# Triangular inverses of a chunked recurrence in packed 32x32 blocks on four row quarters, the inverse and its transpose both by TensorE

## The reference, cut to what matters

```
def _rwkv7_step(state, inp):
    r, w, k, v, kk, kka = inp
    sa = jnp.einsum('dbhvk,dbhk->dbhv', state, kk)
    state = state * w[..., None, :] - sa[..., :, None] * kka[..., None, :] + v[..., :, None] * k[..., None, :]
    y = jnp.einsum('dbhvk,dbhk->dbhv', state, r)
    return state, y
...
    xs = (orient(both(r)), orient(decay), orient(k_dir), orient(both(v)),
          orient(both(kk)), orient(kk[:, :, None, :] * a))
    state0 = jnp.zeros((N_DIRS, B, H, N, N), jnp.float32)
    _, ys = lax.scan(_rwkv7_step, state0, xs)
...
def _dilated_attention(q, k, v, window, dilation):
    s = jnp.einsum('bhrnqd,bhrnkd->bhrnqk', qb, kb).astype(jnp.float32)
    s = jnp.where(valid, s, -jnp.inf)
    m = jnp.max(s, axis=-1, keepdims=True)
    p = jnp.exp(s - m)
```

## Time and profile before

| | us |
|---|---|
| median of 3 runs | 1295.57 (1292.97 to 1296.23) |
| the profiled execution | 1297.45 |
| its span in the profile | 1295.4 |
| TensorE busy in it | 1230.7 |
| the stage: first chunk products to output projection | 917.16 to 1035.03 |

### The profile page before, as it was taken

One profiled execution on the slowest core, in us unless ns is written; L12 is line 12 of the kernel. 1 busy time (PEld: TensorE's weight loads), 2 busy tenths in 40 slices (PEclk: granted clock), 3 DMA queues, 4 the chain that ended last, 5 costly groups with the idle time before them and its releaser, 6 DMA issues.

```text
span 1295.4 us, 27192 instructions
## 1 busy us (share of the span) xinstructions
PE 1230.7 (95%) x11566; PEld 1153.2 (89%) x11566; DVE 586.2 (45%) x1057; ACT 617.9 (48%) x969; POOL 896.1 (69%) x689
## 2 busy tenths in 40 slices
PE   6999799999999999998899999999899988999997
PEld 6999689899998899997899998989898977999996
DVE  2533546742652222224545334458977444432333
ACT  5665434736744444445544445675322014544443
POOL 5988245686986999994799994867400013999992
PEclk9999999999999999999999999989999998999998
DMA  6555134454565556563555655434100022665561
GB/s 247 191 165 179 50 93 139 145 180 146 184 220 165 178 182 190 183 188 115 158 191 184 191 182 194 154 121 157 36 3 3 4 68 66 196 189 185 188 186 66
DMA packets 53256, 189.81 MB, mean 147 GB/s; under 512 B 6160, under 2 KB 7312, under 8 KB 53008
## 3 DMA queue, kind: packets, MB, share of 16 engines
q1 hardware_dynamic: 50256, 181.95, 43.9%
q10 hardware_dynamic: 2880, 6.12, 1.4%
HBM read 187.00 MB, written 1.05 MB: 145 GB/s over the span
## 4 chain that ended last, share of the span: by engine, by line
PE 83%; DVE 9%; ACT 5%; DMA 2%; issue 1%; POOL 0%; DVEq 0%; ACTq 0%
PE product L500 16%; PE product L502 16%; PE product L501 16%; PE bank L557 6%; PE bank L559 6%; PE bank L558 6%; PE product L1036 3%; PE bank L1036 3%; ACT weight_hi L2242 1%; PE product L587 1%; PE product L631 1%; PE bank L500 1%; DVE arena L1504 1%; PE bank L868 1%; PE bank L501 1%
## 5 line engine op out<-in xcount | busy, mean ns | idle before, releaser
L477 POOL TENSOR_TENSOR weight_lo<-raw_ring,weight_hi 128x512 fp32r<-128x512 f32 x684 | 890.6, 1335 | 375.3 <-ACT weight_hi L2242 344.1
L2242 ACT ACTIVATE weight_hi<-raw_ring 128x1024 fp32r<-128x1024 f32 x338 | 356.1, 1059 | 413.4 <-DMA raw_ring<-in_ffn_gu 108.1
L500 PE MATMUL product<-operand_B_hi,weight_hi 128*128 128x256 f32 x1104 | 312.3, 283 | 4.6 <-POOL weight_lo L477 4.6
L502 PE MATMUL product<-operand_B_hi,weight_lo 128*128 128x256 f32 x1104 | 311.3, 282 | 0.0
L501 PE MATMUL product<-operand_B_lo,weight_hi 128*128 128x256 f32 x1104 | 310.8, 282 | 0.0
L500 PE MATMUL product<-operand_A_hi,weight_hi 128*128 128x256 f32 x840 | 242.5, 289 | 14.2 <-DVE weight_lo L1353 10.8
L502 PE MATMUL product<-operand_A_hi,weight_lo 128*128 128x256 f32 x840 | 238.4, 284 | 0.0
L501 PE MATMUL product<-operand_A_lo,weight_hi 128*128 128x256 f32 x840 | 238.3, 284 | 0.0
L500 PEld LDWEIGHTS product<-operand_B_hi,weight_hi 128*128 128x128 f32 x1104 | 208.1, 188 | 7.9 <-issue 3.2
L501 PEld LDWEIGHTS product<-operand_B_lo,weight_hi 128*128 128x128 f32 x1104 | 207.9, 188 | 3.2
L502 PEld LDWEIGHTS product<-operand_B_hi,weight_lo 128*128 128x128 f32 x1104 | 207.9, 188 | 0.0
(11 more groups left out here) (355 smaller groups left out, 1571.1 us busy)
## 6 DMA issues: line engine op xcount, KB each, us to landing
raw_ring<-in_w_in SPq DMA_DIRECT2D x107, 512.0 KB, 3.5
raw_ring<-in_ffn_gu SPq DMA_DIRECT2D x88, 512.0 KB, 3.5
raw_ring<-in_ffn_down SPq DMA_DIRECT2D x44, 512.0 KB, 3.5
raw_ring<-in_w_mlp_up SPq DMA_DIRECT2D x32, 512.0 KB, 4.2
raw_ring<-in_w_mlp_down SPq DMA_DIRECT2D x32, 512.0 KB, 4.2
raw_ring<-in_w_out SPq DMA_DIRECT2D x16, 512.0 KB, 4.2
raw_ring<-in_w_branch_c SPq DMA_DIRECT2D x8, 512.0 KB, 3.4
raw_ring<-in_w_branch_a SPq DMA_DIRECT2D x8, 512.0 KB, 3.4
```

The source lines that it names most:

```text
L477: last = k.nc.gpsimd.tensor_tensor(k.wlo[:, slot, part], k.raw[:, slot, part], k.whi[:, slot, part].bitcast(F32), ALU.subtract)
L500: mm(ps, w_hi, op.hi[:, b, :], start=b == 0, stop=False)
L502: return mm(ps, w_lo, op.hi[:, b, :], start=False, stop=b == blocks - 1)
L2242: k.nc.scalar.activation(k.whi[:, slot, 0:w], k.raw[:, slot, 0:w], ACT.Copy).then_inc(k.s["hi_ready"], 1)
```

## The change

T and its transpose are kept only in their two diagonal 32x32 blocks (`HC` = 32) through levels 1 to 4, packed: partitions 0-31, 32-63, 64-95 and 96-127 hold the two halves of two heads, and a unit has 32 columns (`tc`, `uc` and the new `tt`, 256 columns in all instead of 512). A product of a level is now `quarters`: 8 units x 4 quarters = 32 matmuls of 32x32 by 32 columns. Level 5, which joins the two halves, is two products of `between_halves`, 16 matmuls each. `first_products` makes only one of the two triangular products, in pieces with 32 weight columns (`left_products`, 40 matmuls); the start of `tt` comes from it by a mask (L2108 in the new file) and an addition (L2110), the start of `tc` by a VectorE transpose in 32x32 blocks (L2099). The full 64x64 transpose `ttc`, which `solve` reads, is put together at the end: GpSimd fills it with zeros early, ScalarE copies the diagonal quarters after level 4 (`diagonal_halves`, 4 copies a chunk), VectorE the off-diagonal ones after level 5 (4 copies a chunk). Masks are stored for halves. Apart from that, attention's scores are made with the opposite sign, so that a minimum takes the place of a maximum and its negation, and the exponential has a scale of -1.

```diff
-    k.nt, k.tc, k.uc = ([units(9760 + 1536 * lane + 512 * n) for lane in range(2)] for n in range(3))
+    k.levels_half = k.masks.rearrange("p (d m t) -> p d m t", d=2, m=16)
+    half_units = lambda start: region(start, 8, HC)
+    k.nt = [units(9760 + 1536 * lane) for lane in range(2)]
+    k.tc, k.uc, k.tt = ([half_units(9760 + 1536 * lane + 512 + 256 * n) for lane in range(2)] for n in range(3))
     k.ttc, k.zaac, k.zaqc = ([units((12832, 15904, 18976, 6144)[j] + 512 * n) for j in range(NRC)] for n in range(3))
     k.zaqb = [units((14368, 17440, 20512, 22048)[j]) for j in range(NRC)]
...
+    pool.wait_ge(k.s["cb_made"], 1)
+    for j in range(NRC):
+        k.nc.gpsimd.memset(k.ttc[j], 0.0).then_inc(k.s["tt_zero"], 1)
...
+    def left_products(j):
+        bank = k.lane[j % 2][1]
+        for u in range(8):
+            lhs, rhs = feature(B_, j)(u), feature(A_, j)(u)
+            ahead = 0 if u < 4 else 1
+            for i in (ahead, 1 - ahead):
+                for head in (0, HD):
+                    rows, out = slice(head, head + HD), slice(head + i * HC, head + (i + 1) * HC)
+                    own, other = slice(i * HC, (i + 1) * HC), slice((1 - i) * HC, (2 - i) * HC)
+                    if i == 0 and ahead == 0:
+                        mm(bank[out, u * RC:(u + 1) * RC], lhs[rows, own], rhs[rows, :], start=True, stop=True)
+                    else:
+                        last = mm(bank[out, u * RC:u * RC + HC], lhs[rows, own], rhs[rows, own], start=True, stop=True)
+                        if i == ahead:
+                            last = mm(bank[out, u * RC + HC:(u + 1) * RC], lhs[rows, own], rhs[rows, other],
+                                      start=True, stop=True)
+        return last
+    def quarters(bank, lhs, rhs):
+        for u in range(8):
+            for q in range(4):
+                rows = slice(q * HC, (q + 1) * HC)
+                last = mm(bank[rows, u * HC:(u + 1) * HC], lhs[rows, u, 0:HC], rhs[rows, u, 0:HC], start=True, stop=True)
+        return last
+    def between_halves(bank, lhs, rhs, forward):
+        for u in range(4):
+            for q in range(4):
+                n = u if (q % 2 == 0) == forward else u + 4
+                rows, out = slice(q * HC, (q + 1) * HC), slice((q ^ 1) * HC, ((q ^ 1) + 1) * HC)
+                last = mm(bank[out, n * HC:(n + 1) * HC], lhs[rows, n, :], rhs[rows, n, :], start=True, stop=True)
+        return last
     def first_products(j):
         lane = k.lane[j % 2]
         if j >= 2:
-            pe.wait_ge(s["tt_ev"], 9 + j % 2)
-        per_unit(lane[0], feature(A_, j), feature(B_, j)).then_inc(s["prod_mm"], 1)
-        per_unit(lane[1], feature(B_, j), feature(A_, j)).then_inc(s["prod_mm"], 1)
+            pe.wait_ge(s["tt_off"], 4 * (j - 1))
+        left_products(j).then_inc(s["prod_mm"], 1)
         per_unit(lane[2], feature(B_, j), feature(Q_, j)).then_inc(s["prod_mm"], 1)
     def second_products(j):
         lane = k.lane[j % 2]
-        pe.wait_ge(s["la_ev"], j + 1)
         per_unit(lane[0], feature(C_, j), feature(A_, j)).then_inc(s["prod_mm"], 1)
...
-    def nth(j, level, levels):
-        return 2 * levels * (j // 2) + 2 * (level - 1) + j % 2 + 1
+    def nth(j, level):
+        return 10 * (j // 2) + 2 * level + j % 2 + 1
     def level_left(j, level):
         bank = k.lane[j % 2][1]
+        pe.wait_ge(s["t_ev"], nth(j, level - 1))
         if level == 1:
             pe.wait_ge(s["qc_ev"], j + 1)
-            pe.wait_ge(s["tc_first"], j + 1)
+        if level < 5:
+            quarters(bank, k.nt[j % 2], k.tc[j % 2]).then_inc(s["u_mm"], 1)
         else:
-            pe.wait_ge(s["t_ev"], nth(j, level - 1, 4))
-        per_unit(bank, of(k.nt[j % 2]), of(k.tc[j % 2])).then_inc(s["u_mm"], 1)
+            between_halves(bank, k.nt[j % 2][:, :, HC:RC], k.tc[j % 2], True).then_inc(s["u_mm"], 1)
     def level_both(j, level):
-        lane = k.lane[j % 2]
-        pe.wait_ge(s["u_ev"], nth(j, level, 5))
+        bank = k.lane[j % 2][0]
+        pe.wait_ge(s["u_ev"], nth(j, level - 1))
+        pe.wait_ge(s["tt_ev"], nth(j, level - 1))
         if level == 1:
-            pe.wait_ge(s["ttc_first"], j + 1)
+            pe.wait_ge(s["ac_ev"], j + 1)
+            pe.wait_ge(s["bt_ev"], min(j + 1, NRC - 1))
+            pe.wait_ge(s["ct_ev"], min(j + 1, NRC - 1))
             pe.wait_ge(s["qb_ev"], j + 1)
-            pe.wait_ge(s["ac_ev"], j + 1)
-            pe.wait_ge(s["ct_ev"], min(j + 1, NRC - 1))
-            pe.wait_ge(s["bt_ev"], min(j + 1, NRC - 1))
+        if level < 5:
+            quarters(k.lane[j % 2][2], k.tt[j % 2], k.uc[j % 2]).then_inc(s["t_mm"], 1)
+            quarters(bank, k.uc[j % 2], k.tt[j % 2]).then_inc(s["tt_mm"], 1)
         else:
-            pe.wait_ge(s["tt_ev"], nth(j, level - 1, 5))
-        if level < 5:
-            per_unit(lane[2], of(k.ttc[j]), of(k.uc[j % 2])).then_inc(s["t_mm"], 1)
-        per_unit(lane[0], of(k.uc[j % 2]), of(k.ttc[j])).then_inc(s["tt_mm"], 1)
+            between_halves(bank, k.uc[j % 2], k.tt[j % 2], False).then_inc(s["tt_mm"], 1)
...
-        pe.wait_ge(s["tt_ev"], nth(j, 5, 5))
+        pe.wait_ge(s["tt_diag"], 4 * (j + 1))
+        pe.wait_ge(s["tt_off"], 4 * (j + 1))
         per_unit(k.chain_bank, of(k.ttc[j]), of(k.xs)).then_inc(s["sa_mm"], 1)
...
-            pe.wait_ge(s["tt_ev"], nth(3, 5, 5))
+            pe.wait_ge(s["tt_off"], 4 * NRC)
...
-        nv.scalar_tensor_tensor(sc, k.score_bank[:], HD ** -0.5, wide(k.att_mask), ALU.mult,
-                                ALU.add).then_inc(s["s_ev"], 1)
+        nv.scalar_tensor_tensor(sc, k.score_bank[:], -(HD ** -0.5), wide(k.att_mask), ALU.mult,
+                                ALU.subtract).then_inc(s["s_ev"], 1)
         v.wait_ge(s["s_ev"], h + 1)
-        st.do(nv.tensor_reduce(sm[:, 64 + 2 * h:66 + 2 * h], sc.rearrange("p (i t) -> p i t", i=2), AX_X, ALU.max))
-        st.settle()
-        nv.tensor_scalar(sm[:, 80 + 2 * h:82 + 2 * h], sm[:, 64 + 2 * h:66 + 2 * h], -1.0, None,
-                         ALU.mult).then_inc(s["s_red"], 1)
+        nv.tensor_reduce(sm[:, 80 + 2 * h:82 + 2 * h], sc.rearrange("p (i t) -> p i t", i=2), AX_X,
+                         ALU.min).then_inc(s["s_red"], 1)
...
+    half_bank = lambda bank: bank[:, 0:8 * HC].rearrange("p (u t) -> p u t", u=8)
+    def half_mask(n):
+        return k.levels_half[:, :, n, :].unsqueeze(2).to_broadcast([P, 2, AB, HC])
+    def nth(j, level):
+        return 10 * (j // 2) + 2 * level + j % 2 + 1
+    def turned(j, level):
+        v.wait_ge(s["tt_ev"], nth(j, level))
+        nv.transpose(k.tc[j % 2].rearrange("p u t -> p (u t)"),
+                     k.tt[j % 2].rearrange("p u t -> p (u t)")).then_inc(s["t_ev"], 1)
     def first_products(j):
-        lane = k.lane[j % 2]
-        tc, ttc = k.tc[j % 2], k.ttc[j]
+        lane, tt = k.lane[j % 2], k.tt[j % 2]
         v.wait_ge(s["prod_mm"], products_before(j) + 1)
-        masked(tc, lane[0], 0).then_inc(s["la_ev"], 1)
+        if j >= 2:
+            v.wait_ge(s["tt_diag"], 4 * (j - 1))
+        nv.tensor_tensor(by_way(tt), by_way(units(lane[1])[:, :, 0:HC]), half_mask(0), ALU.mult).then_inc(s["nt_ev"], 1)
+        v.wait_ge(s["nt_ev"], j + 1)
+        nv.tensor_tensor(by_way(tt), by_way(tt), half_mask(5), ALU.add).then_inc(s["tt_ev"], 1)
+        turned(j, 0)
         v.wait_ge(s["prod_mm"], products_before(j) + 2)
-        masked(ttc, lane[1], 0, turned=True).then_inc(s["nt_ev"], 1)
-        v.wait_ge(s["la_ev"], j + 1)
-        nv.tensor_tensor(tc, tc, stack8, ALU.add).then_inc(s["tc_first"], 1)
-        v.wait_ge(s["nt_ev"], j + 1)
-        nv.tensor_tensor(ttc, ttc, stack8, ALU.add).then_inc(s["ttc_first"], 1)
-        v.wait_ge(s["prod_mm"], products_before(j) + 3)
         masked(k.zaqb[j], lane[2], BEFORE_OR_SAME).then_inc(s["qb_ev"], 1)
...
     def level_left(j, level):
-        v.wait_ge(s["u_mm"], nth(j, level, 5))
-        masked(k.uc[j % 2], k.lane[j % 2][1], level).then_inc(s["u_ev"], 1)
+        bank = half_bank(k.lane[j % 2][1])
+        v.wait_ge(s["u_mm"], nth(j, level - 1))
+        if level < 5:
+            nv.tensor_tensor(by_way(k.uc[j % 2]), by_way(bank), half_mask(level), ALU.mult).then_inc(s["u_ev"], 1)
+        else:
+            nv.tensor_copy(k.uc[j % 2], bank).then_inc(s["u_ev"], 1)
     def level_both(j, level):
-        lane = k.lane[j % 2]
+        bank, tt = half_bank(k.lane[j % 2][0]), k.tt[j % 2]
         if level < 5:
-            v.wait_ge(s["t_mm"], nth(j, level, 4))
-            if level == 1:
-                v.wait_ge(s["tc_first"], j + 1)
-            else:
-                v.wait_ge(s["t_ev"], nth(j, level - 1, 4))
-            nv.tensor_tensor(k.tc[j % 2], units(lane[2]), k.tc[j % 2], ALU.add).then_inc(s["t_ev"], 1)
-        v.wait_ge(s["tt_mm"], nth(j, level, 5))
-        if level == 1:
-            v.wait_ge(s["ttc_first"], j + 1)
-        else:
-            v.wait_ge(s["tt_ev"], nth(j, level - 1, 5))
```

(23 more changed lines are left out.)

26 lines of the change are left out of this document (14 added, 12 removed).

## The result

The changed kernel takes 1334.21 us in the median of 4 runs (1329.87 to 1337.75), the one before 1295.55: a ratio of 1.030, 95% interval 1.0276 to 1.0324. The forecast was 1273 us, faster. It was wrong by 61 us and in its sign.

The account below looks back on a forecast made before the run. TensorE, busy 95% of the span, was taken as the bound: 28.0 us gained, less 2.3 for tile shapes and 3.4 for waits, 22.3 net, giving 1273.3 us; range 1266 to 1298, the forecast case's own 1267 to 1280.

Parts of the forecast that it names:

- The unit of cost: TensorE products: 29.2 ns a 64x64 record now, 8.0 ns with four 32x32 quarters side by side; 3328 records, 26.6 us.
- second rival: TensorE fed one record after another, or instruction packets too slow for a level: 1345 or 1330 us; chance 0.18.
- another mechanism: TensorE issue: records of one engine start one after another, at a mean of 29.2 or 25 ns; within the same 0.18.
- 2.3 for shapes: TensorE, where matmul tile shape changes: 16 changes of 0.145 us each, 2.3 us lost.
- Removed: TensorE, four chunks: 64 products of 32 records go, 2048 x 29.2 ns = 59.8 us.
- The left first product: New first product on TensorE, 40 matmuls a chunk with 32 weight columns: 1.3 us each, 5.2 us added.
- New waits: TensorE waiting more for VectorE in the changed stage: four terms, 3.4 us lost in sum, at least 0, doubled 7.
- (a): Stage opening: VectorE paces TensorE, so its saving on the first two chunks is not gained, 1.0 us; block transpose 0.6.
- (c): Stage end: projection waits for eight copies by 32 partitions, 2.1 us against 1.4 of TensorE work: 0.6 us.
- (b): In each level VectorE's 3.8 us of work ends the attention output just as transposes want its bank: 0.2 a level, 1.0.
- (d): Attention's norm chain and the last masked copy before the second levels come later against TensorE: 0.8 us.
- A quarter product of 1.6 to 1.9 us: Sign on TensorE's chain that records are fed one after another; 0.5 us for 64 records would show the forecast right.

Follow-up runs that it names:

- the run with half the instructions: Changed kernel with quarter matmuls' moving side widened from 32 to 64 columns and only every second unit issued: 1282.06 us, ratio 0.9888.
- the run with the first product alone: Kernel before, with only the first product for the inverse's start replaced by VectorE's block transpose of the transposed start: 1291.57 us, ratio 0.996.
- 40 products: Kernel before plus 40 extra constant quarter products, one ahead of each of 40 gate and up tiles of the second FFN: 1329.69 us, ratio 1.0264.
- the first burst in the FFN: Kernel before plus 40 extra constant quarter products in five bursts of eight among the second FFN's gate and up tiles: 1372.82 us, ratio 1.0602.
- the run with four products: Changed kernel, levels 1 to 4 making the inverse by VectorE block transpose, four quarter products a level instead of six: 1301.18 us, ratio 1.0042.

## Why the prediction was wrong

**The step that failed** is "The unit of cost", where it made 8.0 ns a record a rate that 3328 records would keep. Its array part was nearly right: 64 records go from 939.35 to 939.95 us, 9.4 ns each, 37.6 ns a tile where I had 32, and about as much in the FFN (1180.60 to 1181.28 us with the join: 0.68). But a record is two instructions, and in the levels these come at 13.6 to 14.6 ns each, 27 to 29 ns a record. My second rival had that: five packets in 19 us of the earlier trace rows, "one for 3.8 us; a level will need its own in half that time". Its price came out near too, 1345 at 29.2 ns a record and 1330 at 25, but partly by luck: it has every record at that rate and no lower clock, where the runs show stops at some blocks, a block ready at others, and the clock. What I did wrong was to weigh it at 0.18 together with another mechanism, and to argue against it with the earlier trace rows, which show that two loads and two matmuls can begin within 20 ns: true of a few instructions that lie ready, and no evidence on what arrives. The mean of the earlier trace rows, 29.2 ns a record, is 14.6 ns an instruction; the best measured supply is 13.6. While it ran nothing but its 64x64 stream the kernel before had 7% to spare, and I read the number as the array's alone.

**A second term was missing altogether.** Behind the stops the clock fell, and the sum had no term for it. TensorE's busy time in the stage stayed at 115.8 us (114.4 before), though 28.0 less 2.3 for shapes and some 4.3 for 9.4 instead of 8.0 ns (48 products by 0.09) should have gone: 21.4 us. What is left, about 23 us, I put down to the lower clock; it is worked out by difference, and no run took the clock's fall away alone. The sum 34.6 pauses - 21.4 array + 23 clock + 0.7 other idle time = 37, measured 36.6, therefore closes by construction. Another way to the clock's share: in the 78.4 us of the stage that the trace has at the 1.2 GHz level TensorE is busy for 62.7; at the full clock that is an estimated 31 us less, and the kernel before lost some 3 of its own, which leaves 28. So 23 to 28 us, as an estimate. In the run with half the instructions 117.9 - 21.4 + 8.3 = 104.8 meets the measured 104.9, but partly by luck: its double products take 0.55 us and not 0.60, which is 2.6 us more gained, and its clock of 0.90, against 0.97 before, takes some time back.

**Point by point, what held.**
- Removed, 59.8 us at 0.93 a product: the kernel before without 20 of these products should have a stage shorter by 18.6 - 5.5 of waits = 13.1 us, and has one shorter by 11.1: 0.83 us a product in place of 0.93, near enough.
- The left first product: 1.04 us (925.00 to 926.04) at full clock; forecast 1.3. Right side of it, too high.
- New waits: (a) was a cost of 1.0; the run with the first product alone says nothing is lost there. The block transpose takes 0.45 us where I took 0.6 (row below). (c), the projection's wait, was 1.3 us instead of 0.6, since its eight copies took 2.52 us in a row (from 1073.42 us) and not 2.1. (b) can't be read in the changed kernel, where pauses hide it; with half the instructions the levels of chunks 0 and 1 have no wait for VectorE, so 1.0 was too much. (d) is there: the last masked copy and the attention norm are waited for 0.7 us each (L2083, L2065), where the kernel before waited 0.2 and 0.3; 0.8 was right.

```profile
924.69 0.45 DVE L2099 STREAM_TRANSPOSE arena<-arena 128x256 f32<-128x256 f32 x1
```

- A quarter product of 1.6 to 1.9 us was to show the second rival: it took 0.6 at full clock. The sign of this rival was the idle time between products, which I had not listed. I had looked for the fault in the duration of records, and it stood between them.
- Two slips in the working change nothing: the four terms of (b) add up to 3.7, not 3.8, and the chance of faster to 0.73, not 0.72.

**A rule that comes out near the time for another reason.** The Trainium skill's floor of about 25 ns from one matmul's start to the next ("TensorE: Matmul & The Clock Gate", Back-to-back issue gap) would have given some 1330 us. It is not what happened: records start 9.4 ns apart in these tiles while instructions last, and 40 products cost 0.87 us each in the FFN, where 64 x 25 ns would be 1.6.

## What to carry to other kernels

Before cutting matmuls into smaller tiles, count instructions, not only columns: an f32 matmul is four (two loads, two matmuls), and a stretch that wants more than 256 TensorE instructions per 3.5 us will get them no faster, after one block that lies ready. Divide the time that you forecast for the stretch by its instruction count and compare with 13.6 ns: 6.05 us for 804 instructions is 7.5 ns and could not be had; the level before, 8.57 us for 420, is 20.4 ns, and the run that did it in 6 us with as many instructions is at the limit. Where the tuned kernel already stands there, as this one did at the end of its stage, only fewer instructions can help. Here the same idea with fewer instructions, one block transpose on VectorE for each second product, gave 1.0% where smaller tiles lost 3.0%.

## What the runs showed of the hardware

- Instruction supply of TensorE: from one stop to the next, 3.47 us for 256 instructions at best (13.6 ns each) and mostly 3.73, with the DMA engines almost empty (4 GB/s, the levels) or at 84 GB/s (the first burst in the FFN). A burst passes one boundary free and stops at each one after it, 1.5 to 4.2 us. The packet itself is 1.0 us of it (q8's share); how the rest divides between its request and its taking over was not separated.
- Records in four 32x32 tiles side by side: 9.4 ns apart, with 32 moving columns or, from the run with half the instructions, 17 ns with 64.
- Between the first and the last stop of the changed kernel's stage the clock fell to the 1.2 GHz level eight times, each time in, or up to 1.5 us behind, a pause of 1.9 to 2.7 us, and stayed there for longer than the pause. In the run with four products the granted clock is 0.50 from 944.2 to 981.7 us, and the scores stand at 2.07 us from 945 to 976, with one pause of 1.0 us after the first of 1.7. When it comes back, and whether the small tiles' own work helps to keep it down, was not settled.
- 1920 `pe.nop()` were not in the program that ran (27192 instructions and 92 packets of q8, as without them), so they can't be used to load the supply.
